# Attention interleaved with the projection's later chunks, and linear attention with the output projection

## The reference, cut to what matters

```python
proj = rms_norm(h, norm1_g) @ w_in                     # 1024 x 3088
gq, gk, gv, gr, glr, dq, dk, dv = split(proj)
# linear attention, 4 heads: decay from the gate, a state carried from chunk to chunk
log_a = log_sigmoid(glr @ wa2 + ba) / 16;  b = cumsum(log_a)
o = rms_norm(o_intra + o_inter, onorm_g) * silu(gr)
# differential attention, 4 heads of 2 components, causal, relative bias
p = softmax(rms_norm(dq) @ rms_norm(dk).T + bias);  w = p[0] - lam * p[1]
out = rms_norm(w @ dv, subln_g) * (1 - lambda_init)
h = h + concat(o, out) @ w_out
h = h + hier_moe(rms_norm(h, norm2_g))                  # router, then 2 of 32 SwiGLU experts
```

## Time and profile before

| | |
|---|---|
| time, median of 3 runs | 1369.44 us (1368.91 to 1370.79) |
| profiled execution | 1366.81 us, of which the span from first to last instruction is 1365.1 us |
| TensorE busy | 1218.3 us (89%) |
| VectorE busy | 882.5 us (65%) |
| ScalarE busy | 674.5 us (49%) |
| GpSimd busy | 244.5 us (18%) |

### The profile page before, as it was taken

One profiled execution on the slowest core, in us unless ns is written; L12 is line 12 of the kernel. 1 busy time (PEld: TensorE's weight loads), 2 busy tenths in 40 slices (PEclk: granted clock), 3 DMA queues, 4 the chain that ended last, 5 costly groups with the idle time before them and its releaser, 6 DMA issues. The chain is left out here.

```text
span 1365.1 us, 16832 instructions
## 1 busy us (share of the span) xinstructions
PE 1218.3 (89%) x5886; PEld 920.6 (67%) x5887; DVE 882.5 (65%) x1212; ACT 674.5 (49%) x859; POOL 244.5 (18%) x273
## 2 busy tenths in 40 slices
PE   6999999986787877789973899999999999999992
PEld 5888888873554555578862677777777777777771
DVE  4522321115877786543226899999999999999881
ACT  4322221004444443432111777777777777777771
POOL 2023300000223232200002311122221112222110
PEclk9999999996787796889975999999999999999997
DMA  7011012002000001043248799999999999999941
GB/s 269 0 63 62 1 62 93 31 3 80 1 1 1 0 1 62 13 162 124 93 162 330 281 370 376 370 377 380 386 385 378 376 374 380 376 383 382 381 113 24
DMA packets 57183, 262.95 MB, mean 193 GB/s; under 512 B 10852, under 2 KB 15784, under 8 KB 32424
## 3 DMA queue, kind: packets, MB, share of 16 engines
q1 hardware_dynamic: 48808, 239.15, 45.3%
q0 software_dynamic: 7168, 20.98, 6.8%
q10 hardware_dynamic: 1152, 2.10, 0.4%
HBM read 243.32 MB, written 23.07 MB: 195 GB/s over the span
## 5 line engine op out<-in xcount | busy, mean ns | idle before, releaser
L1684 DVE TENSOR_TENSOR experts_w_low<-w_raw,experts_w_high 128x2048 fp32r<-128x2048 f32 x192 | 438.9, 2287 | 64.3 <-ACT experts_w_high L1680 63.9
L1680 ACT CAST experts_w_high<-w_raw 128x2048 fp32r<-128x2048 f32 x192 | 366.0, 1908 | 93.3 <-PE experts_py L1698 52.7
L1696 PE MATMUL experts_ph<-experts_w_high,experts_xT_high 128*96 128x512 f32 x512 | 205.2, 401 | 4.8 <-DVE experts_w_low L1684 3.6
L1697 PE MATMUL experts_ph<-experts_w_low,experts_xT_high 128*96 128x512 f32 x512 | 203.5, 397 | 0.0
L1698 PE MATMUL experts_ph<-experts_w_high,experts_xT_low 128*96 128x512 f32 x512 | 202.4, 395 | 0.0
L1610 POOL DMA_INDIRECT experts_xg<-xn_dram,experts_token x32 | 78.4, 2450 | 382.8 <-DVE experts_token L1590 382.5
L305 PE MATMUL front_pm<-front_w_high,xh 128*128 128x512 f32 x320 | 128.0, 400 | 4.3 <-DVE xl L474 4.3
L305 PE MATMUL front_pm<-front_w_high,xl 128*128 128x512 f32 x320 | 125.7, 393 | 0.0
L305 PE MATMUL front_pm<-front_w_low,xh 128*128 128x512 f32 x320 | 125.7, 393 | 0.0
L1696 PEld LDWEIGHTS experts_ph<-experts_w_high,experts_xT_high 128*96 128x96 f32 x512 | 84.8, 166 | 39.9 <-DVE experts_w_low L1684 3.7
L1698 PEld LDWEIGHTS experts_ph<-experts_w_high,experts_xT_low 128*96 128x96 f32 x512 | 83.3, 163 | 36.7
(11 more groups left out here) (249 smaller groups left out, 1913.4 us busy)
## 6 DMA issues: line engine op xcount, KB each, us to landing
w_raw<-in_moe_w SPq DMA_DIRECT2D x192, 1024.0 KB, 10.4
front_w_raw<-in_w_in SPq DMA_DIRECT2D x12, 1024.0 KB, 7.2
front_x<-in_x SPq DMA_DIRECT2D x8, 512.0 KB, 10.9
outproj_x<-in_x SPq DMA_DIRECT2D x8, 512.0 KB, 4.2
out<-outproj_h SPq DMA_DIRECT2D x8, 512.0 KB, 2.6
xn_dram<-outproj_xn SPq DMA_DIRECT2D x8, 512.0 KB, 2.8
r_dram<-front_qn ACTq DMA_DIRECT2D x8, 256.0 KB, 2.0
rg<-r_dram SPq DMA_DIRECT2D x1, 2048.0 KB, 10.0
```

Source lines behind the costliest of these rows:

```text
L1680: nc.scalar.copy(wh[slot(c)][:], raw[:, u, c, :]).then_inc(w_high, 1)
L1684: nc.vector.tensor_tensor(wl[slot(c)][:], raw[:, u, c, :], wh[slot(c)][:].bitcast(F32), ALU.subtract).then_inc(w_low, 1)
L1696: nc.tensor.matmul(out, x_hi, w_hi, start=start, stop=False)
L1697: nc.tensor.matmul(out, x_hi, w_lo, start=False, stop=False)
```

## The change

Four stages remain: front, mix_out, route, experts.

The front stage now holds the whole of the differential attention. The chunks come in the order gr, dk, dv, dq, gqk, gv, with the gate's product (z) after dk 1. When dq 2 is done (`AHEAD`), attention begins, and the 21 units that are left (dq 3 to 7, gqk, gv) are cut into 168 pieces of three products and handed out evenly over the steps of attention. The items now come by query tile (t = 0 for all four heads, then t = 1, and so on). gr (after silu), gv, gq and gk, and the summed log decay b, go to DRAM. PSUM has one bank for transposes (`pt`), one for values (`po`) and two for units (`pm`); the second component's probabilities have one buffer.

The second stage, `stage_mix_out`, does linear attention and output projection for one tile after another in one loop, with the four tensors (b, q and k, v, r) read back from DRAM by tile into a ring of three. w_out is loaded as chunks 6 and 7 into the slots of the projection's weights; chunk 6 is split during attention.

In the last expert, chunk 3 of the down projection is split and used ahead of chunk 2, which has a slot of its own.

```diff
-MAP = {"dqT": 20, "dkT": 36, "dv": 52, "gv": 68, "gqT": 84, "gkT": 92, "glrT": 219.875, "xh": 148, "xl": 180,
-       "rg": 101,
+MAP = {"dqT": 20, "dkT": 36, "dv": 52, "slot": 68, "xh": 132, "xl": 164,
...
-        stages = [stage_front, stage_mixers, stage_outproj,
-                  stage_route, stage_experts]
+        stages = [stage_front, stage_mix_out,
+                  stage_route, stage_experts]
...
-CHUNKS = [("gv", GV), ("dq", DQ), ("dk", DK), ("dv", DV), ("gr", GRC), ("gqk", GQ)]
+CHUNKS = [("gr", "w_in", GRC), ("dk", "w_in", DK), ("dv", "w_in", DV), ("dq", "w_in", DQ), ("gqk", "w_in", GQ),
+          ("gv", "w_in", GV), ("out", "w_out", 0), ("out", "w_out", 512)]
...
+AHEAD = INDEX["dq", 2] + 1
+N = HD * T
+STEPS = N + 3
...
+    pieces = KD * (len(UNITS) - AHEAD)
+    upto = [min(pieces, pieces * (m + 1) // (STEPS - 1)) for m in range(STEPS)]
+    quota = [upto[m] - (upto[m - 1] if m else 0) for m in range(STEPS)]
...
+        def item(n):
+
+            return n % HD, n // HD
...  TensorE, attention
+            for m in range(STEPS):
+                left = quota[m]
...
+                if m < N:
+                    scores(m)
+                fill(1)
+                if m >= 3:
+                    values(m - 3)
+                for g in range(groups[m - 2] if 2 <= m < N + 2 else 0):
+                    w_transposes(m - 2, g)
+                    fill(1)
+                for i in transposed_in.get(m, []):
+                    if m >= 2:
+                        pe.wait_ge(wT_ready, first[m - 1])
+                    q_transposes(i)
+                fill(left)
...  ScalarE, attention
+            for m in range(STEPS):
+                if m >= 3:
+                    o_square(m - 3)
+                if 2 <= m < N + 2:
+                    copies(m - 2)
+                if m < N:
+                    exps(m)
+                for i in transposed_in.get(m, []):
+                    store_transposed(i)
+                for i in ended_in(m):
+                    if i in q_number:
+                        q_square(i)
+                    else:
+                        spill(i)
+                if m in split_at:
+                    weight_high(*split_at[m])
...  VectorE, attention
+            for m in range(STEPS):
+                if 1 <= m < N + 1:
+                    weights(m - 1)
+                for i in ended_in(m - 1):
+                    if i in q_number:
+                        q_norm(i)
+                if m < N:
+                    maxima(m)
+                if m >= 3:
+                    norm(m - 3)
+                for i in ended_in(m):
+                    if i in q_number:
+                        q_sum(i)
+                if m in split_at:
+                    weight_low(*split_at[m])
...  stage_mix_out, TensorE
+            for n in range(T + 1):
+                if n >= 1:
+                    transposes("o", n - 1)
+                if n < T:
+                    inner(n)
+                else:
+                    transposes("x", n - 2)
+                    router(n - 2)
+                if n >= 1:
+                    products(n - 1, 0)
+                if n < T:
+                    outer(n)
+                    if n >= 2:
+                        transposes("x", n - 2)
+                if n >= 1:
+                    products(n - 1, 1)
+                if 2 <= n < T:
+                    router(n - 2)
...  stage_experts, the tail
-                down(pe, e, 2)
-                down(pe, e, 3)
+                down(pe, e, 3 if tail else 2, first=3 if tail else 2)
+                down(pe, e, 2 if tail else 3, first=3 if tail else 2)
```

More of the change, by code:

```diff
@@ L200, in stage_front, with four @@
+        pm = [ps(f"pm{i}", [P, 512]) for i in range(2)]
+        pt = ps("pt", [P, 4, P])
+        po = ps("po", [P, 512])
+        def four(bank):
+            return bank.rearrange("p (j x) -> p j x", j=4)
+        pm_ahead = [pm[0][:], pm[1][:], score[0][:, 0:512], score[1][:, 0:512]]
+        pt_ahead = [pt[:], four(po[:]), four(score[0][:, 512:1024]), four(score[1][:, 512:1024])]
+        pf = pt[0:HD].rearrange("p j x -> p (j x)")
         x_in = [sem(f"x_in{t}") for t in range(T)]
@@ L227, in _ @@
+        groups = [-(-(item(n)[1] + 1) // 4) for n in range(N)]
+        first = [sum(groups[:n]) for n in range(N + 1)]
         @block.sync
@@ L331, in _, with values @@
+            def values(n):
+                h, t = item(n)
+                pe.wait_ge(wT_ready, first[n + 1])
+                if n >= 1:
+                    pe.wait_ge(o_normed, n)
+                for j in range(t + 1):
+                    last = nc.tensor.matmul(po[:, 0:DDV], wT[:, j, :], dv[:, j, h * DDV:(h + 1) * DDV],
+                                            start=(j == 0), stop=(j == t))
+                last.then_inc(o_ready, 1)
             pe.wait_ge(filled, 4)
```

1635 lines of the change are left out of this document (822 added, 813 removed).

## The result

The changed kernel takes 1333.58 us (median of 4 runs, 1332.42 to 1333.72), the kernel before, run beside it, 1369.18 us (1364.17 to 1370.79). The ratio is 0.9744 with a 95% interval of 0.9718 to 0.9770: 35.6 us less, where 52 were forecast. The profiled execution took 1333.6 us with a span of 1331.9 us, 33.2 us under the span before.

A forecast was written before the change was run, and what follows sets the result against it. TensorE bounds the projections, a chain of latencies between three engines the mixers. Route begins at 191 + 248 + 218 + 8 = 665 against 711 us; less 6 at the tail, 52 us less: 1317 us, range 1272 to 1350.

The forecast's parts named there:

- Stretch 1: Projection ahead of attention: 21 of 48 product units move out, gate products and a bubble are added; 302.5 us becomes 191.
- Stretch 2: Attention with 168 pieces between: eight steps of 54.7 us, times four heads 219 us, plus start, drain, splits and norms: 248 us.
- The term for weight splits: Attention: weight splits of 2.3 us on VectorE in short steps add 4 us.
- The term for q norms: Attention: norms of five dq units stand ahead of the next maxima on VectorE, 5 x 2.2 = 11 us.
- The late chain: Attention from t = 4: wT copies ahead of exponentials make a chain longer than TensorE's work, 7.1 to 9.7 us a step.
- Rival (b): TensorE binds throughout, exponentials and norm hide: attention 220, linear attention with output projection 199, no clock loss, 1262 us; chance 0.20.
- Stretch 3: Linear attention with output projection: lead-in 29 to 30, first cycle 18, six full ones 137, last tile 21, end 12: 218 us.
- 8 of clock: New waits in early attention and once per output tile: 16 us at half clock, costing half where TensorE binds, 8 us.
- Tail: Last expert: TensorE's 7.17 us wait before the hidden transposes shrinks as one chunk is split earlier; 6 us less, at least 3.
- Rival (c): Latencies larger still, from more hand-overs than priced, or half clock twice as often: about 1340 to 1366 us; chance 0.21.
- Rival (d): Slower: attention and the linear attention stage stay at the mixers' 0.78 clock share, some 1394 us; chance 0.06.
- Rival (e): Trips through DRAM (gv, gq, gk, b, r) eat the gain and the time stays the same; chance 0.03.

## Why the prediction was right in kind and 17 us off

**Stretch 1: 191 forecast, 197.9 measured, 6.9 us short.** The units and the added gate products were counted rightly. The missing part is mostly clock. TensorE waits 1.79 us for glr's weights at 69.8 us (0.7 us before) and 1.51 us at the fourth gate product, and after each it runs at half clock, for 3 and for 6 us:

```profile
69.79 0.76 PE L440 MATMUL front_pm<-xh,front_glr_w 128*128 128x512 f32 x1 [1.79 <-DVE front_glr_w L898]
...
94.06 2.07 PE L451 MATMUL front_score<-front_glrT,front_wa 32*128 32x512 f32 x2 [1.51 <-DVEq L820]
96.06 0.80 PE L423 MATMUL front_pm<-slot_high,xh 128*128 128x512 f32 x1
```

The bubble of 1.6 us was forecast in place and size; what follows it was not. Nor is it fixed: the kernel with no piece ahead of the values has both waits, but the first is not followed by half clock and the second by a shorter one (0.93 and not 0.87 from 76 to 100 us), and its attention begins 3.1 us earlier:

```profile
69.71 0.47 PE L440 MATMUL front_pm<-xh,front_glr_w 128*128 128x512 f32 x1 [1.79 <-DVE front_glr_w L897]
```

The last 1.4 us lie between the last dq transposes (196.44) and the first scores (197.87), where TensorE waits 0.83 us for ScalarE's copy.

**Stretch 2: 248 forecast, 248.4 measured, by errors that cancel.** Steps from one item's scores to the next, mean of four: 5.0, 7.9, 5.5, 6.9, 6.4, 7.3, 9.8 us for t = 0 to 6, and 9.2 for t = 7, where 4.4, 5.0, 5.6, 6.1, 7.1, 8.0, 8.8 and 9.7 stood without splits and norms of q. The term for weight splits, 4 us, was at most a third of what they cost (moving them alone gave 13.5): I priced VectorE's 2.3 us of work, and not the 17.6 us that it stands in six places for the cast in front. The term for q norms, 11 us, was too large, by more than half if the medians of the run that moves them (4.7) are taken; VectorE stood 6.7 us in front of them. The late chain was right at the end only: some 0.5 us too long at t = 7, and at t = 4 and 5, where it was to bind with 7.1 and 8.0 us, the steps took 6.4 and 7.3, and taking 0.68 us out of the chain took 0.1 off them. That the sum came out within half a microsecond is luck. Rival (b), TensorE binding throughout, is out: the same products in another order made the steps at t = 7 up to 0.67 us shorter, and with 96 pieces less the time stays. But for t = 4 and 5 it was nearer the truth than the chain.

**Stretch 3: 218 and 8 of clock forecast, 237.3 measured, 11 us short.** The lead-in was 34.7 and not 29 to 30: the barrier took 4.7 us instead of 1, for the spill behind w_out's load, and two instructions of VectorE took some 1.05 us more each beside GpSimd. The first cycle took 20.0 instead of 18, the six full ones 25.1 on average instead of 22.8, the last tile and the end 32.0 instead of 33. In a cycle the stall came out as priced (6.5 us from the last product to the next tile's first, 6.55 measured), again from two errors: the norm took 1.0 us longer, beside GpSimd, and what leads up to it and follows it as much less. The failed step is the clock's: "The new waits are 2.3 us once in 22.8 ... I take 16 us of it, 8 us". Behind the waits of six cycles (the first 4.36 us long, the others 2.63 or 2.64) 54 products ran at half clock, 6 to 13 at a time and 0.2 us each, 11 us in all, and stretch 1 had none in the sum.

**Tail: 6 forecast, 6.3 in the traces and 5.8 by the run that undoes it.**

Rival (c), larger latencies or more half clock, gave 1340 to 1366: half clock and hand-overs above the price are what took the 17 us, less than its range. Rival (d), a granted clock near 0.8 past 191 us, didn't come; but the run with fewer pieces shows how near it lay: at 0.86, with 65 us less to do, the kernel was no faster. Rival (e) fell: past the second stage's first loads (tile 0 and the gain of linear attention) none was waited for. Not settled is how much of the gain each of the two interleavings carries, as neither was undone by itself.

## What to carry to other kernels

When a loop is a chain of latencies between engines, fill TensorE with independent work up to the length of the chain and not inside it: here a kernel with 65 us of products less was no faster, and where the chain bound, one piece of 0.68 us inside it made each step as much longer. Price an instruction in an in-order queue by what it waits for and who stands behind it, not by its length: six splits, priced at 4 us together, gave 13.5 us when they were moved by one step, and two lines swapped on VectorE gave 25. And price a wait of TensorE together with the half clock behind it.

## What the hardware showed that I had not expected

A norm of 128 x 1024 with all operands in SBUF took 2.29 us beside GpSimd's 1.27 us multiplication and 1.28 us without it, and the low parts with a PSUM operand took 1.28 us in both cases. It goes both ways: GpSimd's addition on 128 x 1 elements, 0.22 us elsewhere, took 1.97 us when VectorE's split had begun 0.4 us before it:

```profile
235.69 2.29 DVE L796 TENSOR_TENSOR slot_low<-slot_raw,slot_high 128x2048 fp32r<-128x2048 f32 x1 [2.74 <-ACT slot_high L582]
236.10 1.97 POOL L729 TENSOR_SCALAR front_o_rs<-front_o_ss 128x1 f32<-128x1 f32 x1 [4.74 <-ACT front_o_sq L647]
```

Waits of 2.64 us were followed by half clock once a tile. Of five waits of 1.63 us at the same place one was followed by it and four were not, and the same wait of 1.79 us in stretch 1 was followed by 3 us of it in the changed kernel and by none in another, with the same instructions on both sides. So the length of the wait alone doesn't decide; what else does, these runs don't settle. It also moves times by some 3 us in code that is the same: from 350 to 400 us the granted clock was 0.93 in the changed kernel, with a step of 12.4 us at a weight split, and 1.00 in the kernel with the low part first, with 9.2 us for that step.
